# Row products for shift and scale, a plain first q chunk, gate products taken ahead, and the last output tile split by two engines

## Time and profile before

| | us |
|---|---|
| three timed runs | 3100.67, 3098.56, 3100.30 (median 3100.3) |
| the profiled execution, its own time | 3101.14 |
| its span, first to last instruction | 3099.3 |
| PE busy | 2890.5 (93%) |
| DVE / ACT / POOL busy | 1936.1 / 1324.6 / 1288.6 |
| mean granted TensorE clock | 0.977 |

### The profile page before, as it was taken

The page is one execution under the profiler, slowest core; times in us unless marked ns, Lnnn a source line. Parts: engine busy times, 40 slices in busy tenths (PEclk is TensorE's granted clock), DMA queues, the critical chain, the costliest instruction groups (busy, mean ns, idle before and its releaser), DMA issues. The chain is left out here.

```text
span 3099.3 us, 49908 instructions
## 1 busy us (share of the span) xinstructions
PE 2890.5 (93%) x20118; PEld 1803.1 (58%) x20118; DVE 1936.1 (62%) x3127; ACT 1324.6 (43%) x2346; POOL 1288.6 (42%) x1071
## 2 busy tenths in 40 slices
PE   7989998999979988989799999999998999999998
PEld 7539875884439667864375465564664444444444
DVE  2476897673589996644775665666654564444445
ACT  1353655662366746643344554454542222222222
POOL 1401474000512580002455755756663535555551
PEclk9999999999989999999899999999999999999999
DMA  7323242002201340021011101201122111111111
GB/s 252 130 75 104 93 143 72 12 22 102 92 14 42 123 136 30 18 78 73 27 52 42 69 32 39 82 28 55 55 82 109 55 41 55 44 52 55 43 53 75
DMA packets 50901, 213.50 MB, mean 69 GB/s; under 512 B 4680, under 2 KB 9968, under 8 KB 34032
## 3 DMA queue, kind: packets, MB, share of 16 engines
q1 hardware_dynamic: 42288, 195.63, 17.9%
q10 hardware_dynamic: 8384, 14.68, 1.4%
HBM read 190.36 MB, written 19.94 MB: 68 GB/s over the span
## 5 line engine op out<-in xcount | busy, mean ns | idle before, releaser
L645 POOL TENSOR_TENSOR w_lo<-stage,w_hi 128x512 bf16<-128x512 f32 x340 | 431.4, 1301 | 367.2 <-ACT w_hi L1377 366.8
L638 POOL CAST w_hi<-stage 128x512 bf16<-128x512 f32 x252 | 181.2, 760 | 780.8 <-PE big L285 585.8
L588 POOL TENSOR_TENSOR w_lo<-stage,w_hi 128x512 bf16<-128x512 f32 x180 | 256.3, 1435 | 299.3 <-ACT w_hi L1577 299.3
L283 PE MATMUL big<-w_hi,ht_hi 128*128 128x256 bf16 (+2 forms) x1280 | 354.5, 286 | 15.2 <-DVE arena L1877 4.7
L284 PE MATMUL big<-w_lo,ht_hi 128*128 128x256 bf16 (+2 forms) x1280 | 354.1, 286 | 0.0
L285 PE MATMUL big<-w_hi,ht_lo 128*128 128x256 bf16 (+2 forms) x1280 | 354.0, 286 | 0.0
L283 PE MATMUL big<-ht_hi,w_hi 128*128 128x512 bf16 x800 | 306.4, 383 | 37.2 <-ACT arena L1692 16.5
L284 PE MATMUL big<-ht_lo,w_hi 128*128 128x512 bf16 x800 | 306.3, 383 | 0.0
L285 PE MATMUL big<-ht_hi,w_lo 128*128 128x512 bf16 x800 | 306.0, 383 | 0.0
L283 PE MATMUL big<-arena,w_hi 128*128 128x512 bf16 (+1 forms) x728 | 231.5, 334 | 29.4 <-ACT arena L1591 9.3
L284 PE MATMUL big<-arena,w_hi 128*128 128x512 bf16 (+1 forms) x728 | 230.9, 333 | 0.0
(11 more groups left out here) (393 smaller groups left out, 7200.0 us busy)
## 6 DMA issues: line engine op xcount, KB each, us to landing
stage<-in_w SPq DMA_DIRECT2D x130, 1024.0 KB, 4.8
arena<-in_w_ada SPq DMA_DIRECT2D x48, 512.0 KB, 3.9
arena<-in_x SPq DMA_DIRECT2D x16, 512.0 KB, 7.5
xs<-arena SPq DMA_DIRECT2D x16, 512.0 KB, 2.6
arena<-xs SPq DMA_DIRECT2D x16, 512.0 KB, 7.2
gt<-arena ACTq DMA_DIRECT2D x16, 256.0 KB, 2.6
arena<-gt ACTq DMA_DIRECT2D x16, 256.0 KB, 2.7
out_x<-arena SPq DMA_DIRECT2D x8, 512.0 KB, 2.6
```

The source lines that it names most:

```text
L283: pe.matmul(out, ah, bh, start=start, stop=False, skip_group_check=onto)
L588: return pool.tensor_tensor(lo, x, hi, ALU.subtract)
L638: pool.tensor_copy(w_flat[0][:, w0 + c0:w0 + c1], stage[:, n % RAW_RING, c0:c1]).then_inc(s_w_hi_split, mark(s_w_hi_split, n, q))
L645: ins = pool.tensor_tensor(w_flat[1][:, w0 + c0:w0 + c1], stage[:, n % RAW_RING, c0:c1], w_flat[0][:, w0 + c0:w0 + c1], ALU.subtract)
```

## The change

It makes these edits; the calls that use them follow suit.

- Shift and scale: every piece of `w_ada` is now the moving operand (two 128x512 float32 matmuls a piece, `cb` stationary). The result stands in every partition as a row, and `columns(l, n)` picks the columns with the identity (a DVE product of 128x512 and a sum over 128). It is called four times in the setup, and for layer 1 in slot 5 (n=0) and slot 11 (n=1 to 3); the four layer-1 tiles come from the PSUM pool "c" of three banks. `gate_gain(1)` moves from slot 2 to slot 16, because its load of `g_post` moves behind the last piece.
- Setup order: `con` is loaded second; x comes in two halves (squares, root, scaling); `cb[0]` is made first; the store and reload of the bias row come behind the weights; the small chain for block 2 (`forget_bounds`) runs behind `cb[1]`, its Exp behind `toep_hi`.
- q0 is a plain chunk. ACT reads out f0 earlier, DVE does `forget`, `conv_2(0,0)` and `conv_2(0,1)` ahead of the t1 sums.
- `gates` (gg times mb) and `gated_scan` (ga times the scan) are taken in chunk ma; y2 goes to `IT` for b < 3, and ACT waits for `y2_f` in place of `y2_lo` before f.
- o3 is split by ACT (cast) and DVE (one 128x2048 subtraction), o2 stays with POOL. The ring offsets lose the "+2" and the "first" event.

```diff
-SEVEN = [... and c not in ("xa0", "f0")]
+SEVEN = [... and c not in ("xa0", "f0", "q0")]
-"q": [... for i in range(4)]
+"q": [... for i in (2, 3, 0, 1)]
+            if CHUNKS[n] == (2, "q0"):
+                return 7 * PART, CH
-            return (n + (2 if n >= CHUNK_AT[(2, "o0")] else 0)) % RING * CH, CH
+            return n % RING * CH, CH
...
             sp.dma_start(vec[:, :], AP_["vec"])
+            sp.dma_start(con[:, :], AP_["con"])
             for i in range(4):
                 ada(i)
             for i in range(NT):
                 sp.dma_start(X_TOK[:, i, :], ...)
-                if i < 6:
-                    ada(4 + 2 * i)
-                    ada(5 + 2 * i)
+                if i % 2:
+                    ada(3 + i)
+                    ada(4 + i)
+            for i in range(12, 16):
+                ada(i)
             for n in range(RAW_RING):
                 weights(n)
...
-                    if n < 4:
-                        for q in range(4):
-                            ins = pe.matmul(g[:, (n * 4 + q) * 8 + k:...], ada_buf(i)[:, k % 2, q * P:(q + 1) * P], s_(S_C + k), start=True, stop=True)
-                    else:
-                        ins = pe.matmul(g[:, (n - 4) * 512:(n - 3) * 512], cb[l][:, k, :], ada_buf(i)[:, k % 2, :], start=k == 0, stop=k == KT - 1)
+                    ins = pe.matmul(g, cb[l][:, k, :], ada_buf(i)[:, k % 2, :], start=k == 0, stop=k == KT - 1)
...
+            def columns(l, n):
+                dve.wait_ge(s_ada_used, when(s_ada_used, l * 32 + 4 * n + 3))
+                step(dve.tensor_tensor(own, g.rearrange("p (q c) -> p q c", q=4), ident.unsqueeze(1).broadcast_to((P, 4, P)), ALU.mult))
+                step(dve.tensor_reduce(s_(S_T + 4 * n, 4), own, AX.X, ALU.add))
...
+            columns(0, 0)
+            scale_x(0)
+            columns(0, 1)
+            scale_x(1)
+            columns(0, 2)
+            columns(0, 3)
+            gains(0)
...
# ACT, b == 0
+                    forget_0(0)
                     parts_high(SEVEN[0], (0, 1, 2))
+                    sums_to_tt(1, "t2")
                     parts_high(SEVEN[0], (3, 5))
+                    forget_0(1)
                     parts_high(SEVEN[0], (4,))
+                    sums_to_tt(1, "t3", "t4")
                     parts_high(SEVEN[0], (6,))
+                    evac(QE[0], ACT.Silu, "q", 0, 0)
+                    act.wait_ge(s_gemm, when(s_gemm, "q", 0, 1))
+                    for g in range(2):
+                        sums_to_tt(g, "t1")
+                    evac(QE[1], ACT.Silu, "q", 0, 1)
# ACT, b > 0
-                    for m in range(2):
-                        act.wait_ge(s_hgrn_dve, when(s_hgrn_dve, "y2_lo", b - 1, m))
-                    seven("f", b, ACT.Copy, u1=lambda: y2_store(b - 1))
+                    act.wait_ge(s_hgrn_dve, when(s_hgrn_dve, "y2_f", b - 1, 0))
+                    seven("f", b, ACT.Copy, u2=lambda: act.wait_ge(... "y2_f", b - 1, 1), p5=lambda: y2_store(b - 1))
# DVE, b == 0
                     sums_2(0)
                     sums_2(1)
-                    dve.wait_ge(s_gemm, when(s_gemm, "f", 0, 1))
-                    for g in range(2):
-                        sum_low(g, "t1", TSB[g])
-                    conv_2(0, 0)
-                    seven("q", 0, c22=(lambda: forget(0, 0),), c12=(lambda: forget(0, 1),))
-                    conv_2(0, 1)
+                    forget(0, 0)
+                    forget(0, 1)
+                    conv_2(0, 0)
+                    conv_2(0, 1)
+                    dve.wait_ge(s_gemm, when(s_gemm, "q", 0, 1))
+                    for g in range(2):
+                        sum_low(g, "t1", TSB[g])
# DVE, chunk ma
-                seven("ma", b, hgrn, c11=(lambda: gated_state(b, 0),))
+                seven("ma", b, hgrn, c11=(lambda: gates(b, 0), lambda: gated_state(b, 0)), c22=(lambda: gates(b, 1), lambda: gated_scan(b, 0)), c12=(lambda: gated_scan(b, 1),))
             recurrent(3, 0)
+            dve.wait_ge(s_cv_hi, when(s_cv_hi, CHUNK_AT[(2, "o3")], PIECES - 1))
+            dve.tensor_tensor(w_flat[1][:, w0:w0 + CH], stage[:, n % RAW_RING, :], w_flat[0][:, w0:w0 + CH], ALU.subtract)
             normed_state(3, 1)
```

More of the change, by code:

```diff
@@ L55 @@
 STRASSEN = range(3, 16)
-SEVEN = [n for n, (l, c) in enumerate(CHUNKS) if l == 2 and c[:-1] in B_CHUNKS and c[:-1] != "ri" and c not in ("xa0", "f0")]
+SEVEN = [n for n, (l, c) in enumerate(CHUNKS) if l == 2 and c[:-1] in B_CHUNKS and c[:-1] != "ri" and c not in ("xa0", "f0", "q0")]
 SEVEN_AT = {n: k for k, n in enumerate(SEVEN)}
@@ L1112, in _ @@
                     seven("f", b)
-                seven("q", b)
+                    seven("q", b)
                 def hgrn(c, st):
@@ L1771, in _ @@
                 seven("ma", b, ACT.Sigmoid, hgrn, p5=y2_load_rest if b == 3 else None)
+            n = CHUNK_AT[(2, "o3")]
+            act.wait_ge(s_w_in[n % RAW_RING], when(s_w_in[n % RAW_RING], n))
+            for sem, value in used_by(n) if events else ():
+                act.wait_ge(sems[sem], value)
+            for q in range(PIECES):
+                c0 = span(n)[0] + q * CH // PIECES
+                act.activation(w_flat[0][:, c0:c0 + CH // PIECES], stage[:, n % RAW_RING, q * CH // PIECES:(q + 1) * CH // PIECES], ACT.Copy).then_inc(s_cv_hi, mark(s_cv_hi, n, q))
             reciprocal_root(3, 1)
@@ L1949, in _ @@
             dve.tensor_copy(GSL[3][:, 8:16], v_("norm_mlp", 0, 8)).then_inc(s_dve_setup, mark(s_dve_setup, "gain", 3))
-            E_, Z_, Z2, PL = [SCOL[:, 32 + 8 * i:40 + 8 * i] for i in range(4)]
-            dve.tensor_tensor(LB, v_("lb", 0, 8), v_("lb", 0, 8), ALU.subtract).then_inc(s_dve_setup, mark(s_dve_setup, "lb_d"))
-            dve.wait_ge(s_act_setup, when(s_act_setup, "lam_exp"))
-            step(dve.tensor_scalar(Z2, E_, 2.0, None, ALU.add))
-            step(dve.reciprocal(Z2, Z2))
@@ new lines, in scale_x @@
+            def scale_x(half):
+                dve.wait_ge(s_rms, when(s_rms, "x", 0, half))
+                step(dve.reciprocal(s_(S_RSTD2 + 4 * half, 4), s_(S_RSTD2 + 4 * half, 4)))
+                for i in range(4 * half, 4 * half + 4):
+                    dve.tensor_scalar(X_TOK[:, i, :], X_TOK[:, i, :], s_(S_RSTD2 + i), None, ALU.mult).then_inc(s_xn, mark(s_xn, 0, i))
+            columns(0, 0)
[3 more added lines that the diff above has]
+            columns(0, 2)
@@ L2131, in beside @@
                         gate_gain(0)
+                    if l == 0 and slot == 5:
+                        columns(1, 0)
+                    if l == 0 and slot == 16:
                         gate_gain(1)
@@ L2138, in beside @@
                         if l == 0:
-                            ada(1)
+                            for n in range(1, 4):
+                                columns(1, n)
+                            gains(1)
                         conv_pad()
```

225 lines of the change are left out of this document (122 added, 103 removed).

## The result

| | before | after |
|---|---|---|
| median of four runs, us | 3100.45 | 3046.55 (3045.51 to 3047.23) |
| ratio to before, 95% interval | | 0.9827, 0.981 to 0.9844 |
| the profiled execution, its span | 3101.14, 3099.3 | 3046.43, 3044.6 |
| mean granted TensorE clock | 0.977 | 0.98 |

The account below looks back on a forecast made before the run. The PE is busy 93% of the span, so only its waits or half-clock stretches can pay. From 3101.1, -26 + 2 - 11 - 13.5 - 11 = -59.5 gives 3041.6, hence 3041 measured; range 3020 to 3060.

Parts of the forecast that it names:

- Setup: Setup: row products at 2.4 GHz replace 54.8 us of column products, PE then waits for gate piece 16; 26 us gained.
- Search: Layer 0's search: columns calls show 0.7 us in slot 11, gate_gain(1) 1.22 us in slot 16; 2 us lost.
- Start of block 2: Block 2's start: f0 read out earlier, wait before q0 gone, first level of v0 earlier; 11 us gained.
- a sign that I was wrong: Block 2's start: the prediction would be wrong if v0 began later than q0's end.
- Turns: Three turns between b's: f's u1 copied earlier, POOL starts q 4.5 us earlier each time; 13.5 us gained.
- Output projection: Output projection: wait for o3 gone as ACT and DVE split it, first tile added at 2359.5; 11 us gained.
- The tail: After the output projection: what follows is PE-bound and shifts along; 0 us.
- A: Rival, setup: PE stays at 1.2 GHz during the loads because pieces leave gaps; price 14 us, 3055; chance 0.12.
- B: Rival: block 2's start and turns give half, t1 and POOL's chain replacing removed waits; 3054; chance 0.14.
- C: Rival: better than forecast, fewer gaps in the loads and less contention; 3022; chance 0.11.
- D: Rival: slower than before, columns' identity product and sum costing about 10 us a call or more; 3108 at 11; chance 0.03.
- E: Rival: PE reabsorbs every gain because another wait ends at the old place; within 0.2% of 3100; chance 0.02.

Follow-up runs that it names:

- u_start: Changed kernel with the start of block 2 undone: q0 in seven products, f0 read out late, t1 sums first, old ring places; 3051.14 us.
- s_parts: Changed kernel with chunk q started once its first low part is there, the PE waiting part by part and POOL making part 4 earlier; 3034.18 us.
- before_banks: Kernel before the change with one edit: the half banks of q's seven products in the order 2, 3, 0, 1; 3093.02 us.
- s_defer: Changed kernel with conv_2(0,1) and forget(0,1) moved into chunk v0, xs_high(1) behind u2, q0's second tile read ahead of the t1 casts; 3045.76 us.
- combined: Changed kernel with s_load, s_parts, gate_gain(1) in slot 23, conv_2(0,1) in two halves and forget(0,1) in v0, xs_high(1) behind p5; 3020.59 us.
- setup_columns: Changed kernel with layer 0's shift and scale as one-column products again, the new load order kept; 3054.86 us.
- t_wait: Changed kernel with ACT again waiting for both y2_lo ahead of chunk f and storing y2 behind u1, gate products left in chunk ma; 3046.34 us.
- u_start2: As u_start, but with the half banks of q0's seven products in the order 2, 3, 0, 1; 3056.65 us.
- s_load: Changed kernel with gate pieces 16 and 17 loaded ahead of the second weight chunk, 18 and 19 ahead of the gate rows; 3041.79 us.

## Why the prediction was right

- **Setup** (-26, measured -24.0). Right: the products at 2.4 GHz, x's scaling hidden, the PE waiting for the gate piece 16 (8 us forecast, 7.1 measured) and 24.3 us from it to the first big matmul (24.6). The PE began 0.9 us earlier than I had it and was at 2.4 GHz from 9.6 us, not 13; in eleven runs with row products that point lies between 9.4 and 12.7. The loads were worse: three gaps, 2.70 us the longest, and behind that one 3.4 us at half clock, which I had not counted, so that the products ended at 43.3 and piece 16 came at 51.44, for 42 and 50. That is the mis-sized term, 1.4 us of the 2; the rest is the second gate piece and the transposes at half clock (0.4) and rounding.
- **Search** (+2, measured +2.4). The call of 1.4 us and the 0.7 us that show in slot 11 held. The other term did not: I had DVE's chain carry `gate_gain(1)` to the PE, and overlooked the wait of 1.90 us that DVE has in slot 23 in before, which swallows it. What came in its place is 1.6 us of half clock behind the PE's wait in front of slot 12, so the total is right partly by luck. From slot 0 to slot 30 u_start takes 177.25 us, before 176.63: without the half clock the search costs 0.6.
- **Start of block 2** (-11, measured -10.6). The total held, with errors that cancel and with luck: 1.4 us of it are the clock at xa0's start, which I did not forecast. DVE's sums ended at 1506.0, 4 us earlier than 1532.5 less 22.4. The t1 subtractions took 4.38 us and not 2.4, and `forget` 8.3 and not 7. v0 did not begin at q0's end, which I had named as a sign that I was wrong: it waited 3.1 us for ACT's readout of q0. That step of the mechanism failed; it cost nothing, since v0 waited 4.4 us more for the t1 sums later. And one of the reasons was incomplete: the 16.5 us before q0 were a matter of which bank q0 begins with.
- **Turns** (-13.5, measured -11.6). f's u1 was copied at 1695.25, which is 1728.65 on the old scale (1728.5 forecast), and POOL started on q 4.4 us earlier (4.5 forecast). The term missed is POOL's chain: 17.1 us long, where I carried over 16.2; with it the sum is 3 x (4.4 - 0.9) = 10.5. DVE's conv_2 and adds lie beside it now; that they cause it was not tried alone. I did not separate the two edits. The experiments do: the products carry it. On the PE a part of the gain is clock: in the three turns the granted clock is 0.50 for 20.5 us in before and for 6.8 us after the change.
- **Output projection** (-11, measured -10.6). DVE's subtraction of o3 took 3.24 us (2.2 to 4.3), the last `y2_low` ended at 2312.0 (2357.0 on the old scale, 2356.6 forecast), the PE waited 1.5 us for it (1.3), and the first tile was added at 2314.85 (2359.9, 2359.5). I named the split as the cause; the moved products are one too.
- **The tail** (0, measured +0.9): DVE's final operation on the last tile (L2724) waits 0.65 us for a store to free its buffer.

The rivals: A (1.2 GHz throughout the loads) fell, L681 costs 1.8 us a piece but for its start and the two pieces behind the gap. B's half gains fell, though its mechanism, POOL's chain in place of the removed wait, is what bounds the turns. C (3022) fell: the loads had more gaps than forecast, and the contention that DVE was spared in the sums came back in `forget` and t1. D fell: `columns` costs 1.44 us a call and not 10. E fell.

## What to carry to other kernels

A PE wait is a wait for the last of several things: a chunk's seven subtractions, a tile's second bank. Ask which of them the first instruction needs; waiting for that alone (s_parts) or giving it the bank that is free first (before_banks) cost a few lines and gave 10 and 6.5 us by the medians. Where an engine's backlog bounds a stage, moving it behind the wait needs care for what stands there: in front of the next level's operations it gained nothing (s_defer); cut in two, with those operations between the halves, and with one ACT operation moved too, 8.6 us (combined). Before a gain or loss of 1 to 2 us is put down to an edit, compare the granted clock of the same stretch in both: here 1.6 us of the search and 1.4 us of block 2 were clock. And undo edits one by one: the two at the turns looked like one mechanism, and one of them was worth nothing beside the other.

## What was not expected of the hardware

- 55 us of one-column matmuls without a gap leave the PE at 1.2 GHz: the 512-column piece behind them takes 3.43 us in setup_columns. With the operands' roles changed the level is at 2.4 GHz from 9.6 us, 3.0 us behind the first piece (up to 6.0 in the other runs), and a piece takes 1.8 us. The profile's PEclk column reads 1.00 up to its first clock record (81.03 us in before, 66.96 in setup_columns, 9.61 in the changed kernel), whatever the durations are; so up to there the level has to be read from durations. Behind it the column agrees with them.
- DVE and POOL slow each other, but less than if one stood still for the other's whole instruction. In the changed kernel's sums of block 2:

```profile
1483.89 2.07 DVE L2399 TENSOR_TENSOR arena<-arena,ht_lo 128x1024 f32<-128x1024 f32 x1
...
1502.41 1.23 DVE L2410 TENSOR_TENSOR arena<-arena,ht_lo 128x1024 f32<-128x1024 f32 x1
```
```profile
1678.76 1.26 POOL L606 TENSOR_TENSOR stage<-stage 128x512 f32<-128x512 f32 x1
...
1698.60 2.06 POOL L606 TENSOR_TENSOR stage<-stage 128x512 f32<-128x512 f32 x1
```

  Alone they take 1.23 and 1.26 us, beside each other 2.07 and 2.06. The Trainium skill (SBUF — State Buffer, Who interferes with whom) has the loser blocked for the whole instruction; in turns that would be 1.23 + 1.26 = 2.49 for each. The traces show 2.1.
- The DMAs brought the setup's loads at up to 407 GB/s where SP had enough queued; in the changed kernel (the last two columns are DMA share and GB/s):

```profile
20.00:25.00 5.00, 2.99 (x5) 1.35 (x6) 1.47 (x3) 3.21 (x6) 0.00 (x0) 0.83 1.04 407
```

  The 358 GB/s per core that the Trainium skill gives for loads from HBM (DMA: Bandwidth & Descriptors, Where 436 GB/s comes from) are passed here too, as in the earlier trace rows.
- The nine profiles with one and the same setup differ by 2.8 us in the first big matmul and by 8.5 us in the start of xa0, though the medians of the changed kernel and t_wait, which do the same at every stage, are 0.2 us apart. A difference of 5 us between two single profiles of this kernel says nothing unless it is counted from the start of its own stage. Where such profiles differ in the same code, they differ in time at half clock: from slot 30 to xa0, u_start2 has 44.4 us at a granted clock of 0.50 and takes 1041.6 us, s_load has 61.4 us and takes 1047.1. A wait ahead of a stretch does not decide it alone: the 3.25 us in front of xa0 are followed by half clock in seven of these traces, before's among them, and by full clock in seven.
